# A fused two-block transformer kernel: attention outputs one step later, three probability buffers, and the filler units of the first attention in pairs

## The reference, cut to what matters

```python
def masked_softmax(s, mask):
    s = jnp.where(mask, s.astype(jnp.float32), NEG)
    m = jnp.max(s, axis=-1, keepdims=True)
    e = jnp.where(mask, jnp.exp(s - m), 0.0)
    return e / jnp.maximum(jnp.sum(e, axis=-1, keepdims=True), 1e-30)
...
        s_c = jnp.einsum('bqghd,bcgd->bghqc', qb, kcc) * scale
        p_c = masked_softmax(s_c, cmp_end[None, :] <= t[:, None])
        o_c = jnp.einsum('bghqc,bcgd->bqghd', p_c.astype(vcc.dtype), vcc)
...
        sc = (jnp.einsum('bqhd,bkhd->bhqk', qn, k_nope)
              + jnp.einsum('bqhd,bkd->bhqk', qr, k_r)) * scale
        p = masked_softmax(sc, kpos[None, :] <= t[:, None])
        o = jnp.einsum('bhqk,bkhd->bqhd', p.astype(v.dtype), v)
...
        mixed = (jax.nn.sigmoid(gate_a) * (o_a @ w_o_nsa[l])
                 + jax.nn.sigmoid(gate_b) * (o_b @ w_o_mla[l]))
```

## Time and profile before

| what | us |
|---|---|
| median of 3 runs | 2789.37 (2788.86 to 2789.41) |
| the profiled execution, its own time | 2788.05 |
| its span | 2786.3 |
| TensorE busy (PE) | 2771.9, 99% of the span |
| VectorE (DVE), ScalarE (ACT) busy | 1496.8 (54%), 1229.0 (44%) |
| mean granted TensorE clock | 0.999 |

### The profile page before, as it was taken

How to read it: one execution, slowest core, us unless ns; L and a number is a source line. 1 busy time by engine, 2 the same in 40 slices (tenths; PEclk the granted TensorE clock), 3 DMA queues, 4 the chain that set the end, 5 groups by cost and what they waited for, 6 DMA issues and landing times.

```text
span 2786.3 us, 30416 instructions
## 1 busy us (share of the span) xinstructions
PE 2771.9 (99%) x13185; PEld 2308.9 (83%) x13185; DVE 1496.8 (54%) x1215; ACT 1229.0 (44%) x1293; POOL 14.8 (1%) x28
## 2 busy tenths in 40 slices
PE   9999999999999999999999999999999999999999
PEld 7888778888888888888888888888888888888887
DVE  5455764455465445455455684665555455544555
ACT  5335664345554343343444544444433333333453
POOL 0000000000000000000000000000000000000000
PEclk9999999999999999999999999999999999999999
DMA  7745036555455565555556654545655555566555
GB/s 235 218 146 165 31 118 204 192 192 200 166 181 186 193 195 182 196 183 194 186 192 205 201 182 152 180 160 182 215 187 194 189 189 187 192 195 196 172 183 174
DMA packets 256437, 508.15 MB, mean 182 GB/s; under 512 B 8162, under 2 KB 18992, under 8 KB 255408
## 3 DMA queue, kind: packets, MB, share of 16 engines
q1 hardware_dynamic: 254112, 495.61, 54.2%
q0 software_dynamic: 2016, 10.36, 1.1%
q10 hardware_dynamic: 176, 0.23, 0.0%
HBM read 504.08 MB, written 2.10 MB: 182 GB/s over the span
## 4 chain that ended last, share of the span: by engine, by line
PE 98%; DVE 1%; ACT 1%; issue 0%; DVEq 0%; ACTq 0%
PE acc L679 30%; PE acc L680 30%; PE acc L684 30%; PE tb L665 2%; PE acc L945 1%; ACT prob L1588 1%; PE tb L996 0%; PE tb L961 0%; DVE negmax L2071 0%; PE acc L887 0%; PE acc L884 0%; PE acc L886 0%; PE tb L1163 0%; PE tb L809 0%; PE acc L924 0%; PE acc L897 0%
## 5 line engine op out<-in xcount | busy, mean ns | idle before, releaser
L1838 DVE TENSOR_TENSOR wlo<-raw,whi 128x2048 fp32r<-128x2048 f32 (+1 forms) x465 | 1063.9, 2289 | 862.1 <-ACT whi L1345 861.2
L1345 ACT ACTIVATE whi<-raw 128x2048 fp32r<-128x2048 f32 (+1 forms) x465 | 889.3, 1914 | 982.7 <-PE acc L684 777.1
L679 PE MATMUL acc<-whi,ahi 128*128 128x512 f32 (+1 forms) x1968 | 767.0, 391 | 0.4 <-DVE alo L1930 0.4
L680 PE MATMUL acc<-whi,alo 128*128 128x512 f32 (+1 forms) x1968 | 761.6, 388 | 0.0
L679 PE MATMUL acc<-whi,bhi 128*128 128x512 f32 x1528 | 596.8, 391 | 0.0
L680 PE MATMUL acc<-whi,blo 128*128 128x512 f32 x1528 | 594.6, 389 | 0.0
L684 PE MATMUL acc<-wlo,ahi 128*128 128x512 f32 (+1 forms) x1968 | 484.1, 387 | 0.0
L679 PEld LDWEIGHTS acc<-whi,ahi 128*128 128x128 f32 x1968 | 370.3, 188 | 75.1 <-DVE wlo L1927 0.9
L680 PEld LDWEIGHTS acc<-whi,alo 128*128 128x128 f32 x1968 | 370.4, 188 | 73.9
L684 PEld LDWEIGHTS acc<-wlo,ahi 128*128 128x128 f32 x1968 | 367.2, 188 | 75.4
L684 PE MATMUL acc<-wlo,bhi 128*128 128x512 f32 x1528 | 377.8, 389 | 0.0
(11 more groups left out here) (339 smaller groups left out, 1559.3 us busy)
## 6 DMA issues: line engine op xcount, KB each, us to landing
raw<-in_w_ff SPq DMA_DIRECT2D x128, 1024.0 KB, 5.2
raw<-in_w_in SPq DMA_DIRECT2D x119, 1024.0 KB, 5.1
raw<-in_w_gate SPq DMA_DIRECT2D x44, 1024.0 KB, 5.1
raw<-in_w_up SPq DMA_DIRECT2D x44, 1024.0 KB, 5.1
raw<-in_w_down SPq DMA_DIRECT2D x44, 1024.0 KB, 5.0
raw<-in_w_out SPq DMA_DIRECT2D x16, 1024.0 KB, 5.2
raw<-in_w_o SPq DMA_DIRECT2D x16, 1024.0 KB, 5.1
raw<-in_w_ple_gate SPq DMA_DIRECT2D x16, 1024.0 KB, 5.0
```

The source lines that it names most:

```text
L679: nc.tensor.matmul(out_(t), hi[:, kt, tt(t)], whi[:, slot, wc(k)], start=first and k == 0, stop=False)
L680: nc.tensor.matmul(out_(t), lo[:, kt, tt(t)], whi[:, slot, wc(k)], start=False, stop=False)
L1345: nc.scalar.activation(whi[:, g % SPLIT, 0:n_], raw[:, g % RAW, 0:n_], ACT.Copy).then_inc(w_hi, 1)
L1838: V.tensor_tensor(wlo[:, g % SPLIT, 0:n_], raw[:, g % RAW, 0:n_], whi[:, g % SPLIT, 0:n_].bitcast(F32), ALU.subtract).then_inc(w_lo, 1)
```

## The change

It sets `DEPTH` to 4 and a new `MID` to 2. TensorE's end(m) comes four steps after its front instead of three; the middle stays two steps after it. `prob` and `probT` get a third buffer each (`prob3`, `probT3`), taken in turn; `pc_s`, `pc` and `pcT` move to other addresses for that. ACT takes the exponential of m ahead of the copy of the transposes of m-2, and DVE the scale of m-1 ahead of its copy of m-2. The filler table puts units in pairs: two at steps 0 and 2, two at the attn of pair 1 (selected), pair 0 (window) and pair 1 (latent), and two in each of the two steps behind the last item. The sum stays 32. Steps that had one unit each, and all steps in between, have none.

```diff
+        prob3 = sb("prob3", [P, 2, CAUSAL], F32, B_AT + 5 * KB)
+        probT3 = sb("probT3", [P, 2, CAUSAL], F32, B_AT + 28 * KB)
+        p_of = lambda p: prob[:, p % 3 - 1] if p % 3 else prob3
+        pT_of = lambda p: probT[:, p % 3 - 1] if p % 3 else probT3
...
-            plan = {m: 1 for m in calls[0] if m < 2 or items[m]["kind"] != "prep"}
             last = calls[0][-1]
-            for m in (last - 15, last - 16, last - 10, last - 6):
-                del plan[m]
-            plan.update({2: 2, 4: 2, last + 1: 1, last + 2: 1})
+            plan = {0: 2, 2: 2, last + 1: 2, last + 2: 2}
+            for m in calls[0]:
+                it = items[m]
+                if it["kind"] == "attn" and (it["pair"], it["br"]) in ((1, 1), (0, 2), (1, 0)):
+                    plan[m] = 2
...
-        DEPTH = 3
+        MID, DEPTH = 2, 4
...
                     if ms[0] <= m - deep:
                         end_of(m - deep)
-                    if ms[0] <= m - deep + 1 <= ms[-1]:
-                        middle_of(m - deep + 1)
+                    if ms[0] <= m - MID <= ms[-1]:
+                        middle_of(m - MID)
                     fill(FILL.get(m, 0))
...
                     if m - DEPTH in calls[0] and group_end(m - DEPTH):
                         o_out(m - DEPTH)
...
+                    if m in calls[0]:
+                        front_of(m)
+                    probs_of(m - back)
...
-                    for step, k in ((middle_of, m - deep + 1), (scale_of, m - 1)):
+                    for step, k in ((scale_of, m - 1), (middle_of, m - MID)):
```

More of the change, by code:

```diff
@@ L321, in build @@
         rtmp2 = nc.alloc_sbuf_tensor_at("rtmp2", [P, 4, HEADS * ROPE // 2], F32, offset=base + B_AT + 28 * KB)
-        pc_s = nc.alloc_sbuf_tensor_at("pc_s", [P, TT, HPG, NC], F32, offset=base + B_AT + 4 * KB)
-        pc = nc.alloc_sbuf_tensor_at("pc", [P, TT, HPG, 32], F32, offset=base + B_AT + 5 * KB)
-        pcT = nc.alloc_sbuf_tensor_at("pcT", [P, TT, P], F32, offset=base + B_AT + 6 * KB)
+        pc_s = sc("pc_s", [TT, HPG, NC])
+        pc = nc.alloc_sbuf_tensor_at("pc", [P, TT, HPG, 32], F32, offset=base + B_AT + 4 * KB)
+        pcT = nc.alloc_sbuf_tensor_at("pcT", [P, TT, P], F32, offset=base + B_AT + 31 * KB)
         grows = nc.alloc_sbuf_tensor_at("grows", [P, P], F32, offset=base + P_AT + 4 * KB)
@@ L1543, in o_rounded, with front_of @@
                 last.then_inc(o_hi, 1)
+            def front_of(m):
+                it = items[m]
+                s = acc[bank(m)]
+                f = it.get("fam")
+                if it["kind"] == "prep":
+                    n = 2 * SEQ if (f, it["what"]) == ("nsa", "k") else 4 * SEQ
+                    d = DHEAD[f]
+                    scale = d ** -0.5 if it["what"] == "q" else 1.0
+                    k0 = 0
+                    if (f, it["what"]) == ("nsa", "k"):
+                        k0 = KS_AT
+                        if it["g"] == 0:
+                            act.wait_ge(cmp_end, 1)
+                        nc.scalar.activation(kT[0:d, it["slot"], KC_AT:KS_AT],
+                                             kccT[:, it["g"] * NC:(it["g"] + 1) * NC], ACT.Copy)
+                    act.wait_ge(front, fronts(m))
+                    nc.scalar.activation((qT if it["what"] == "q" else kT)[0:d, it["slot"], k0:k0 + n],
+                                         s[0:d, 0:n], ACT.Copy, scale=scale).then_inc(prep_done, 1)
+                elif it["kind"] == "cmp":
+                    act.wait_ge(cmp_sub, it["n"] + 1)
+                    nc.scalar.activation(pc_s[:, :, :, :], pc_s[:, :, :, :], ACT.Exp).then_inc(cmp_exp, 1)
+                elif it["kind"] == "attn":
+                    act.wait_ge(max_done, it["n"] + 1)
+                    p = it["p"]
+                    for n in range(2):
+                        for t in range(TT):
+                            bs = [b for b, (tq, _) in enumerate(BLOCKS[f]) if tq == t]
+                            at, end = bs[0] * P, (bs[-1] + 1) * P
+                            c0, c1 = score_cols(it, t)
+                            last = nc.scalar.activation(
+                                p_of(p)[:, n, at:end], s[:, n * COLS + c0:n * COLS + c1], ACT.Exp,
+                                bias=negmax[:, p % 2, n * TT + t:n * TT + t + 1],
+                                accum_out=sums[:, p % 4, n * TT + t:n * TT + t + 1])
+                    last.then_inc(exp_done, 1)
@@ L1545, in attend, with probs_of @@
+            def probs_of(m):
+                if m in calls[0] and items[m]["kind"] == "attn":
+                    f, p = items[m]["fam"], items[m]["p"]
+                    act.wait_ge(pt_done, items[m]["n"] + 1)
+                    nc.scalar.activation(pT_of(p)[:, 0, :], tb[0][:, 0:len(BLOCKS[f]) * P],
+                                         ACT.Copy).then_inc(pts_done, 1)
             def attend():
-                back = DEPTH - 1
+                back = MID
                 for m in range(calls[0][0], calls[0][-1] + 1 + back):
@@ L1551, in attend @@
                         o_out(m - DEPTH)
[L1552 to L1592, removed]
@@ L2126, in scale_of @@
                 for t in range(TT):
-                    x = prob[:, p % 2, :, t * P:(2 * t + 1) * P]
+                    x = p_of(p)[:, :, t * P:(2 * t + 1) * P]
                     last = V.tensor_tensor(x, x, r[:, :, t:t + 1].to_broadcast([P, 2, (t + 1) * P]), ALU.mult)
@@ L2135, in middle_of @@
                     dve.wait_ge(pt_done, it["n"] + 1)
-                    V.tensor_copy(probT[:, p % 2, 1, :], tb[0][:, COLS:COLS + len(BLOCKS[f]) * P]).then_inc(ptv_done, 1)
+                    V.tensor_copy(pT_of(p)[:, 1, :], tb[0][:, COLS:COLS + len(BLOCKS[f]) * P]).then_inc(ptv_done, 1)
                 elif it["kind"] == "cmp":
@@ L2166, in attend @@
                 ms = calls[0]
-                deep = DEPTH
-                for m in range(ms[0], ms[-1] + 1 + deep):
+                for m in range(ms[0], ms[-1] + 1 + MID):
                     if m <= ms[-1]:
                         front_of(m)
-                    for step, k in ((middle_of, m - deep + 1), (scale_of, m - 1)):
+                    for step, k in ((scale_of, m - 1), (middle_of, m - MID)):
                         if k in ms:
```

4 lines of the change are left out of this document (2 added, 2 removed).

## The result

| | median us | lowest | runs |
|---|---|---|---|
| before | 2789.03 | 2787.69 | 18 |
| the change | 2794.95 | 2793.53 | 18 |

The ratio is 1.0022, with a 95% interval from 1.0016 to 1.0029: the change makes the kernel 5.9 us slower. The forecast was 2793.5 within 2786.0 to 2797.0. Its likeliest case was a loss of 4.1 us, and the measured one lies 0.3 us beyond the 5.6 us that I had drawn as the bound to "no change".

The account below looks back on a forecast made before the run. The prediction took TensorE, busy for 99% of the span, as the bound, with unchanged work; seven wait items summed to 12.5 us against 8.4 before, +4.1, giving 2793.5 us within 2786.0 to 2797.0.

Parts of the forecast that it names:

- likeliest case: Whole kernel: waits in the first attention grow, +4.1 us; 2791 to 2795 by rounding, chance 0.48.
- The bound and the work: First attention: TensorE bounds it, matmuls stay the same in number and size, pairing units saves nothing; work term zero.
- Item 1: Front(5): three units ahead of it are gone, leaving 2.74 us of wait where 0.65 were.
- Item 2: Fronts 12, 19, 26: 0.33 us each from missing units, more at two behind DVE's moved half conversion; 3.6 us together.
- Item 3: Cmp transposes at steps 8, 15, 22, 29 wait for ACT's copy, now behind an exponential; 1.8 us together.
- Item 4: Middles of 14, 21, 28 wait for a scale behind the next item's row maximum on DVE; 1.2 us together.
- Items 5 and 6: Latent items 37 and 41: 1.2 us of wait; tail, middle of 42 waiting for ACT's copy: 1.6 us.
- Item 7: Small waits: second query prep on the first one's copy, 0.2 us, and twice 0.1; 0.4 us together.
- The sum: All seven items in the first attention: 12.5 us of waits against 8.4 before, +4.1 us.
- Rival B: Clock falls to half behind the hole ahead of front(5), one fall costing at most 1.7 us: +5.8, 2795.2; chance 0.17.
- own signs of being wrong: First attention stage shorter than 124 or longer than 130 us, or the clock under 1.00 in it.
- Rivals A and C: A: deeper pipeline hides queueing, -3.5 us, 2785.9, chance 0.13; C: waits only move, within 2 us of 2789.4, chance 0.17.

Follow-up runs that it names:

- e7: The change with three filler units between front(3) and front(5), taken from step 2 (one) and step 5 (two); 2792.59 us.
- e5: The change with DVE's second half of each weight conversion one step later, behind the row maximum of items 10, 24 and 40; 2792.76 us.
- e4: The change with 11 additional matmuls (some 2.4 us, result overwritten) filling TensorE's wait ahead of front(5); 2793.25 us.
- e12: The change with DVE's old order in every step, copy of m-2 ahead of the scale of m-1; 2795.11 us.
- e10: e8 with DVE's softmax and scale reordered around the cmp item, and ACT copying ahead of the exponential in steps 5 and 43; 2786.56 us.
- e8: The change with the edits of e5 and e7, both output roundings one step later, and five filler units moved to other steps; 2789.71 us.

## Why the prediction was right, and where it was not

- **The bound and the work.** Right. The same matmuls take the same time at full clock (115.7 us of work in the stage before and 115.0 in the change, by a count that closes to 0.7), and two units in a row cost two units. Nothing behind the attention moved.
- **Item 1, the hole at front(5).** 2.74 forecast, 2.79 found. e7 puts three units back and it is 0.63.
- **Item 2, fronts 12, 19, 26.** 1.72, 0.33 and 1.56 forecast; 1.65, 0.31 and 1.22 found. e5 shows the conversion's part.
- **Item 3, the cmp transposes.** 1.02 and three times 0.26 forecast; at full clock (e4) 0.90 and three times 0.21 to 0.23. In the change the first was hidden by the slow clock.
- **Item 4, the middles behind the cmp item.** This term was mis-sized. I had three waits of 0.40 for the scale, at the middles of 14, 21 and 28, and each is about 0.8; in the change the middle of 7 waits 1.06 on top, at full clock (e4) 0.13. The step that failed is "wait for a scale that DVE takes behind the row maximum": the middle of such an item also waits for the copy of the cmp transposes, which DVE now takes behind that scale. The semaphore stands in the code; I had left it out of the working. The rows of DVE and TensorE in the change, with 311.40 the middle of 14:

```profile
309.90 1.02 DVE L2140 TENSOR_TENSOR prob<-prob,rinv 128x256 f32<-128x256 f32 x2
310.84 0.42 DVE L2151 COPY pcT<-tb 128x256 f32<-128x256 f32 x1
```

```profile
311.40 0.85 PE L966 MATMUL tb<-con,prob 128*128 128x128 f32 x6 [0.76 <-DVE pcT L2151]
```

  How long after its scale such a middle starts, when nothing else holds it, shows in e12:

```profile
308.91 1.03 DVE L2140 TENSOR_TENSOR prob<-prob,rinv 128x256 f32<-128x256 f32 x2
```

```profile
310.00 0.88 PE L966 MATMUL tb<-con,prob 128*128 128x128 f32 x6 [0.66 <-DVE prob L2140]
```

  That is 1.09. In the change the scale alone would so have let the middle of 14 start at 310.99, 0.41 before it did. Of its 0.82, half is the scale's, as forecast, and half the copy's. No run has the copy behind the middle, so the split is worked out and not tested.
- **Items 5 and 6.** 1.2 and 1.6 forecast, 1.2 and 1.5 found.
- **Item 7.** 0.4 forecast, about half of it found: the second query prep waits 0.2 behind the key prep in the change, and 0.1 in e4.
- **The sum.** +4.1 forecast for the waits; with the clock held (e4) the kernel is 4.2 us over before. That it fits to 0.1 us is partly luck: item 4 came out 1.4 us higher and items 2 and 3 together 0.7 lower, and a count of waits closes only to about half a microsecond.
- **Rival B.** This is what came on top, and I gave it 0.17. Its sum was +5.8 us, and +5.9 was measured; the price of the fall was put at 1.7, and the medians of the change and e4 differ by 1.7. The forecast's own signs of being wrong were a stage of over 130 us or a clock under 1.00 in it, and the stage is 131.45 us at 0.97. So the number came in range, inside the 2791 to 2795 of my likeliest case too, while the case itself did not hold: the step that took the clock to stay at 1.00 was wrong, and it is luck that its price fitted in. The mean clock speaks for a fall in every run: it is 0.998 in 13 of them and 0.997 in 4, and in e4, the same kernel with the hole filled, 0.999 in 10 of 11. A mean does not tell where the clock fell; the one profiled execution does. I weighed against it that the 0.65 hole of before had left the clock alone, though the new hole is four times as long. The Trainium skill (TensorE: Matmul & The Clock Gate, on how gaps bite in real kernels) shows a kernel whose clock falls in waits of about 3 to 5 us between its bursts of matmuls. The traces here agree that gaps do it, and go further: a fall followed each hole of 2.1 us or more, and all of these holes but one were under 3.
- **Rivals A and C.** Both fell by the time, 2785.9 and within 2 us of 2789.4 against 2794.95. What recovered the time (e5, e7 to e10) is order and placement alone; no run takes the third buffers away by themselves, so what they are worth is not shown.

## What to carry to other kernels

A pipeline one step deeper only removes the waits whose releaser is a step behind; work that was moved behind something else in an in-order queue, or filler that had covered a latency loop, comes back as a wait. Most of these waits could be written down beforehand from start-to-start distances, to 0.1 us in three of the seven items here and to 0.4 in three more; in the seventh I had not followed every semaphore that the instruction waits for. Filler belongs inside the loops whose latency exceeds the work between two users of a bank, and the longest hole deserves the first units, since it can cost the clock as well as itself. Half-step jobs like a weight conversion did best here behind the short operation that others wait for and not right ahead of it (e5). And a wait closed at one place can open at the next of the same chain, as in e7, e8 and e10: only the stage as a whole tells what was won.

## What the runs showed of the hardware that I had not expected

Behind which holes the clock fell. Over the traces of the thirteen changed kernels the granted clock of the attention fell to 0.50 behind holes of 2.10 (twice), 2.34, 2.79 (six times), 2.91 and 3.2 us, and never behind one of 1.72 us or less (there are over a dozen between 1 and 1.72). These are one trace for each kernel, with nothing between 1.72 and 2.10, and the earlier trace rows show a fall with no hole at all, so this is no threshold for other kernels.

The stay at half clock was 3.41 us at every one of these falls but that of the change, where it was 6.82. There the fall began at 274.52, 0.18 us before the hole ended; in the ten other cases it began 0.07 to 1.31 us behind the hole's end. Whether that is the reason for the longer stay, no run here tells.
